# Streamed activation tiles of five matmul stages placed in groups at different 32-byte steps relative to the weight tiles

## What is computed

```python
def trunk_layer(...):
    h = rmsnorm(x, norm_mix)
    z = h @ w_in                      # projections of mixers A, B, C and of the merge gates
    o_a = dsa_attention(...); o_b = moba_attention(...); o_c = retention(...)
    m = (jax.nn.sigmoid(g_a) * (o_a @ w_pa) + jax.nn.sigmoid(g_b) * (o_b @ w_pb)
         + jax.nn.sigmoid(g_c) * (o_c @ w_pc))
    x = x + m @ w_out
    f, c_new = conv_ffn(rmsnorm(x, norm_ffn), cprev, ffn_up, ffn_gate, conv_w, conv_b, ffn_down)
    x = x + f

def conv_ffn(...):
    u, g = h @ ffn_up, h @ ffn_gate
    # c: causal convolution of width 3 over u
    y = (jax.nn.gelu(c, approximate=False) * g) @ ffn_down
```

## The kernel before

| jobs | weights | streamed | chunks x jobs | triples |
|---|---|---|---|---|
| pa | w_pa | oa_hi, oa_lo | 8 x 16 | 128 |
| pb | w_pb | ob_hi, ob_lo | 8 x 16 | 128 |
| out | w_out | m_hi, m_lo | 16 x 16 | 256 |
| d1 | ffn_down | y_hi, y_lo | 22 x 16 | 352 |
| d2 | ffn_down | y_hi, y_lo | 21 x 16 | 336 |

## Time and profile before

### The profile page before, as it was taken

How to read it: one execution, slowest core, us unless ns; L and a number is a source line. 1 busy time by engine, 2 the same in 40 slices (tenths; PEclk the granted TensorE clock), 3 DMA queues, 4 the chain that set the end, 5 groups by cost and what they waited for, 6 DMA issues and landing times.

```text
span 2383.5 us, 44504 instructions
## 1 busy us (share of the span) xinstructions
PE 2351.6 (99%) x17202; PEld 2270.1 (95%) x17202; DVE 1410.9 (59%) x2095; ACT 919.1 (39%) x1274; POOL 314.0 (13%) x629
## 2 busy tenths in 40 slices
PE   8999999999999999999999999999999999999997
PEld 8978999999999999998999999999999999999997
DVE  6535568989987545445456645666654356666443
ACT  5334444333333444334333344333333333333332
POOL 1135110000002322333200011000000000000001
PEclk9999999999999999999999999999999999999999
DMA  7448645546557988998776544444445544444553
GB/s 239 143 132 243 178 140 182 180 168 207 204 175 264 307 290 292 302 336 298 245 265 194 183 151 148 153 153 149 152 151 153 150 157 154 148 153 154 149 153 106
DMA packets 174434, 458.69 MB, mean 192 GB/s; under 512 B 25018, under 2 KB 74538, under 8 KB 174096
## 3 DMA queue, kind: packets, MB, share of 16 engines
q1 hardware_dynamic: 141040, 372.31, 47.9%
q0 software_dynamic: 26128, 75.67, 9.7%
q10 hardware_dynamic: 7056, 7.88, 0.9%
HBM read 425.27 MB, written 27.52 MB: 190 GB/s over the span
## 4 chain that ended last, share of the span: by engine, by line
PE 95%; DVE 2%; ACT 1%; issue 1%; DMA 0%; DVEq 0%; SPq 0%; ACTq 0%
PE ps L789 87%; PE ps L1061 1%; PE ps L1014 1%; PE ps L860 1%; PE ps L1044 1%; ACT w_hi L1102 1%; DMA xT<-in_x 0%; PE ps L984 0%; PE ps L976 0%; PE ps L872 0%; PE ps L927 0%; PE ps L963 0%; PE ps L967 0%; PE ps L824 0%; PE ps L902 0%
## 5 line engine op out<-in xcount | busy, mean ns | idle before, releaser
L1353 DVE TENSOR_TENSOR w_lo<-w_raw,w_hi 128x1024 fp32r<-128x1024 f32 (+1 forms) x622 | 749.4, 1207 | 778.3 <-ACT w_hi L1102 775.3
L789 PE MATMUL ps<-h_hi,w_hi 128*128 128x320 f32 x3696 | 1160.6, 314 | 11.7 <-DVE w_lo L1353 9.5
L789 PE MATMUL ps<-h_lo,w_hi 128*128 128x320 f32 x3696 | 1132.3, 306 | 0.0
L789 PE MATMUL ps<-h_hi,w_lo 128*128 128x320 f32 x3696 | 1125.8, 305 | 0.0
L1102 ACT ACTIVATE w_hi<-w_raw 128x1024 fp32r<-128x1024 f32 (+1 forms) x622 | 647.4, 1043 | 802.2 <-PE ps L789 790.5
L789 PEld LDWEIGHTS ps<-h_hi,w_hi 128*128 128x128 f32 x3696 | 694.7, 188 | 41.9 <-issue 38.9
L789 PEld LDWEIGHTS ps<-h_lo,w_hi 128*128 128x128 f32 x3696 | 694.9, 188 | 0.4
L789 PEld LDWEIGHTS ps<-h_hi,w_lo 128*128 128x128 f32 x3696 | 694.5, 188 | 0.0
L789 PE MATMUL ps<-y_hi,w_hi 128*128 128x320 f32 x688 | 213.5, 310 | 1.7 <-DVE yt L1425 1.7
L789 PE MATMUL ps<-y_lo,w_hi 128*128 128x320 f32 x688 | 210.5, 306 | 0.0
L789 PE MATMUL ps<-y_hi,w_lo 128*128 128x320 f32 x688 | 209.2, 304 | 0.0
(11 more groups left out here) (322 smaller groups left out, 2063.4 us busy)
## 6 DMA issues: line engine op xcount, KB each, us to landing
w_raw<-in_w_in SPq DMA_DIRECT2D x258, 512.0 KB, 5.0
w_raw<-in_ffn_up SPq DMA_DIRECT2D x86, 512.0 KB, 3.9
w_raw<-in_ffn_gate SPq DMA_DIRECT2D x86, 512.0 KB, 3.7
w_raw<-in_ffn_down SPq DMA_DIRECT2D x80, 448.0 KB, 3.4
kpg<-in_cache_b_k SPq DMA_DIRECT2D x128, 128.0 KB, 4.5
vpg<-in_cache_b_v POOLq DMA_DIRECT2D x128, 128.0 KB, 5.0
kpg<-in_cache_a_k SPq DMA_DIRECT2D x128, 128.0 KB, 4.8
vpg<-in_cache_a_v POOLq DMA_DIRECT2D x128, 128.0 KB, 4.9
```

The costliest lines, as they stand in the source:

```text
L789: mm = mmul(bank[q][:, 0:T], wp[:, s, cols], xp[:, x.k0 + k, :], start=(x.first and k == 0 and t == 0), stop=(x.last and k == x.nk - 1 and ...
L1353: tt(w_lo[:, s, 0:n], w_raw[:, s, 0:n], w_hi[:, s, 0:n].bitcast(F32), ALU.subtract).then_inc(w_lo_done, 1)
```

## The change

The tiles `oa`, `ob`, `m` and `y`, high part and rest, are no longer one tile each. Each is cut along k into groups (lots), and each group starts at a place of its own; a table `STEPS` gives for each group its chunks and the places of high part and rest. A helper `stepped` moves the start up to the next byte offset with the wanted place, allocates the group, and hands back a list of the chunks by k, which the matmuls and the makers of the chunks index. The weights and `h_hi`/`h_lo` stay where they are.

`oa_hi`, `oa_lo`, `ob_hi` and `ob_lo` are now made by two instructions of 1,280 elements each in place of one of 2,560. All other instructions keep their order and sizes. `x1`, `ost`, `sq`, `sqa`, `term` and the tables of the ConvFFN move by the bytes that the gaps take.

```diff
+STEPS = {"m": (((0, 6), 64, 0), ((6, 11), 96, 32), ((11, 16), 32, 32)),
+         "oa": (((0, 4), 64, 96), ((4, 8), 64, 32)),
+         "ob": (((0, 4), 96, 96), ((4, 8), 32, 96)),
+         "y": (((0, 5), 96, 0), ((5, 10), 32, 0), ((10, 16), 0, 96), ((16, 22), 0, 32))}
...
+        assert R % 128 == 0
+
+        def stepped(src, part, start, end):
+
+            by_k, by_lot = [], []
+            for (k0, k1), *steps in STEPS[src]:
+                start += (steps[part] - start) % 128
+                name = f"{src}_{('hi', 'lo')[part]}{k0}"
+                x = at(start, end)(name, [P, k1 - k0, T], F32R)
+                start += 4 * T * (k1 - k0)
+                by_k += [x[:, k, :] for k in range(k1 - k0)]
+                by_lot.append((k0, k1, x[:, :, :]))
+            return by_k, by_lot, start
...
-        oa_hi, oa_lo = ro("oa_hi", [P, 8, T], F32R), ro("oa_lo", [P, 8, T], F32R)
-        misc_at = ro.at - R
-        ob_hi, ob_lo = ro("ob_hi", [P, 8, T], F32R), ro("ob_lo", [P, 8, T], F32R)
-        x1_at = ro.at - R
-        x1 = ro("x1", [P, KD, T])
+        oa_hi, oa_hi_lots, end = stepped("oa", 0, ring_at + 32, 109376)
+        oa_lo, oa_lo_lots, misc_at = stepped("oa", 1, end, 109376)
+        ob_hi, ob_hi_lots, end = stepped("ob", 0, misc_at, 109376)
+        ob_lo, ob_lo_lots, x1_at = stepped("ob", 1, end, 109376)
+        x1 = at(x1_at, x1_at + 20480)("x1", [P, KD, T])
...
-        m_hi = at(0, 20480)("m_hi", [P, KD, T], F32R)
-        m_lo = at(ring_at + 32, ring_at + 20512)("m_lo", [P, KD, T], F32R)
-        rq = at(109376, 114496)
+        m_hi, _, _ = stepped("m", 0, 0, 20832)
+        m_lo, _, end = stepped("m", 1, ring_at + 32, misc_at + 512)
+        rq = at(x1_at + 20480, x1_at + 25600)
...
-        y_hi = at(0, 28160)("y_hi", [P, KF1, T], F32R)
-        y_lo = at(28160, 56320)("y_lo", [P, KF1, T], F32R)
-        rf = at(misc_at, x1_at)
+        y_hi, _, y_mid = stepped("y", 0, 0, misc_at)
+        y_lo, _, _ = stepped("y", 1, y_mid, misc_at)
+        rf = at(misc_at + 512, x1_at)
...
-                            mm = mmul(bank[q][:, 0:T], wp[:, s, cols], xp[:, x.k0 + k, :],
+                            mm = mmul(bank[q][:, 0:T], wp[:, s, cols], xp[x.k0 + k],
...
-                fn((oa_hi, ob_hi)[m][:, :, :], ost[:, m, :, :], ACT.Copy).then_inc(rounded, 1)
+                for k0, k1, x in (oa_hi_lots, ob_hi_lots)[m]:
+                    ins = fn(x, ost[:, m, k0:k1, :], ACT.Copy)
+                ins.then_inc(rounded, 1)
...
-                tt((oa_lo, ob_lo)[m][:, :, :], ost[:, m, :, :], (oa_hi, ob_hi)[m][:, :, :].bitcast(F32), ALU.subtract)\
-                    .then_inc(split, 1)
+                for (k0, k1, lo), (_, _, hi) in zip((oa_lo_lots, ob_lo_lots)[m], (oa_hi_lots, ob_hi_lots)[m]):
+                    ins = tt(lo, ost[:, m, k0:k1, :], hi.bitcast(F32), ALU.subtract)
+                ins.then_inc(split, 1)
```

More of the change, by code:

```diff
@@ L391, in build @@
         W = {n: a[n] for n in ("w_in", "w_pa", "w_pb", "w_pc", "w_out", "ffn_up", "ffn_gate", "ffn_down")}
-        X = {"h": (h_hi, h_lo), "oc": (h_hi, h_lo), "h2": (h_hi, h_lo), "oa": (oa_hi, oa_lo), "ob": (ob_hi, ob_lo),
+        by_k = tuple([x[:, k, :] for k in range(KD)] for x in (h_hi, h_lo))
+        X = {"h": by_k, "oc": by_k, "h2": by_k, "oa": (oa_hi, oa_lo), "ob": (ob_hi, ob_lo),
              "m": (m_hi, m_lo), "y": (y_hi, y_lo)}
@@ L1110, in evacuated @@
                     act.wait_ge(m_done, job.n + 1)
-                    fn(m_hi[:, job.n, :], m_f[:, job.n, :], ACT.Copy).then_inc(rounded, 1)
+                    fn(m_hi[job.n], m_f[:, job.n, :], ACT.Copy).then_inc(rounded, 1)
                 elif job.kind == "out":
@@ L1119, in evacuated @@
                     act.wait_ge(bank_free, j + 1)
-                    fn(y_hi[:, job.n % KF1, :], yt[:, job.n % 2, :], ACT.Copy).then_inc(rounded, 1)
+                    fn(y_hi[job.n % KF1], yt[:, job.n % 2, :], ACT.Copy).then_inc(rounded, 1)
                 elif job.kind == "d2":
@@ L1436, in later @@
                     dve.wait_ge(rounded, BEFORE["m"] + n + 1)
-                    tt(m_lo[:, n, :], m_f[:, n, :], m_hi[:, n, :].bitcast(F32), ALU.subtract).then_inc(split, 1)
+                    tt(m_lo[n], m_f[:, n, :], m_hi[n].bitcast(F32), ALU.subtract).then_inc(split, 1)
                 elif job.kind == "up":
@@ L1458, in later @@
                     i = n % KF1
-                    tt(y_lo[:, i, :], yt[:, n % 2, :], y_hi[:, i, :].bitcast(F32), ALU.subtract).then_inc(split, 1)
+                    tt(y_lo[i], yt[:, n % 2, :], y_hi[i].bitcast(F32), ALU.subtract).then_inc(split, 1)
             def dense(n):
```

## The result

The changed kernel takes 2390.65 us (median of 14 runs, 2389.57 to 2391.87) where the kernel before, run beside it on the same chip, takes 2385.52 us. The ratio is 1.0022, with a 95% interval of 1.0015 to 1.0029: slower, by 5.1 us (0.2%). The forecast had +1.1 us; the measured time lies inside the stated range, on the side of the slower rival.

A forecast was written before the change was run, and what follows sets the result against it. TensorE's matmul pace was taken as the bound. Terms 1.2 - 0.2 - 0.2 + 0.25 = +1.1 us on the profiled 2383.5 gave 2384.6, with 1.6 us around the span 2386.2 us; stated range 2381 to 2392 us.

The forecast's parts named there:

- slower rival: Streaming from 32 or 96 is itself bad, costing 8 us in d1, d2, out and pa: 2393.5 us; chance 0.24.
- That only relative places count: For all matmuls, cost depends on the streamed tile's place less the loading weights' place; no separate size.
- The price by pairs: Each matmul of y, m, oa costs c(d), d being streamed place less loading place; c from 143.8 to 147.1 ns.
- the new groups contain no d outside these four: Place differences d in the new groups are only 0, 32, 64 or 96, so the old trace can price them.
- The term for y: In d1 and d2, four groups of y, 688 triples at 433.3 ns before, sum to +1.2 us.
- that for m: In out, three groups of m, 256 triples at 436.7 ns before, sum to -0.2 us.
- that for oa: In pa, two groups of oa, 128 triples at 440.0 ns before, sum to -0.2 us.
- the sign that the prediction gave itself: In the changed timeline, one group over 3 ns a triple from its predicted pace would show the rule wrong.
- the bounds of the gaps: Outside pb, 1,616 matmuls streaming from 32 or 96: -8 us at a gap of 0.14, +8 us at 0.15.
- Additivity: In every stage a triple costs the sum 2 c(d_hi) + c(d_lo), fixed by its places; 433.3 to 440.0 ns before.
- The cover of pb: In pb, VectorE and ScalarE set 3.64 us a unit, so ob's groups count nothing; -0.3 us without that.
- The cut instructions: Four more instructions making oa and ob delay a TensorE unit by 0.25 us, bounds 0 and 0.5 us.

The follow-up runs named there:

- run with other places: Changed kernel with another set of group places for y, m, oa and ob; no total time given, y's groups took 438.8, 444.7, 439.9 and 444.3 ns a triple.
- first map: Changed kernel with each w_hi slot 32 bytes further than the last, w_lo at 128 modulo 256, and y, m, oa, ob in 15 groups; 2405.29 us.

## Why the prediction was right or wrong

**What bounds the kernel** was right: TensorE's pace, read from starts. The 5.4 us are its paces and one late unit.

**That only relative places count** was right (the move of everything). The slower rival had the sign, and +8.3 us where 5.1 came, but a wrong mechanism: a tile at 32 or 96 is not bad by itself. Its 0.24 rested on a reason that one run removes.

**The price by pairs failed**, and the step that failed is the sentence "the new groups contain no d outside these four". It holds modulo 128. The place counts modulo 256, and there eight differences are possible; of y's four groups none had both parts at a difference seen before. The term for y was 1.2 us and measured 3.85, that for m -0.2 and measured +1.25, that for oa -0.2 and measured 0. What misled was that four values of d for three equations looked like a full table, while in the kernel before the streamed tiles all lay in one half of 256 bytes and the weights in the other, so that nothing in its trace could tell 128 from 256. By the sign that the prediction gave itself, a group over 3 ns from its price, the rule is wrong in six groups of eleven (five up, one down). The forecast's own range should have reached to the bounds of the gaps from the start.

**Additivity**, the other assumption, fails as well: a triple at one and the same placement has no one price. In the run with other places, y's first group (96 above w_hi, 128 above w_lo, modulo 256) runs all of job 2 of d1 at 433.3 ns with gaps of 148, 140 and 146 ns, and job 4 of d2 at 440.0 ns with 147, 146 and 147, at identical places. The first map shows the same in units of h, and there the gaps of the triple just ahead go with the pace that follows. That what runs ahead decides is the reading of this; no run varied it alone. A table of prices by place can't hold it.

**The cover of pb held.** Its stretch took 57.5 us before and after, though ob's groups moved by -0.1 and -6.6 ns a triple.

**The cut instructions** cost 0.22 to 0.23 us for the 0.25 of the sum.

**The rule of the Trainium skill** (page "TensorE: Matmul & The Clock Gate", section "Step-by-step: what each phase is for") says that loading the next tile's weights takes no read bandwidth from the running matmul. The prediction's reading of it, that all places would be alike, is refuted: pa takes 440.0 or 433.3 ns a triple by its distance to the weight tiles. So the load and the stream are not independent here; whether it is read bandwidth that is lost, no run shows.

**The size.** That the stated range held the time is luck as far as the mechanism goes: it had been stretched into rivals of which neither was true. The forecast's own range, 2384 to 2388.5, did not hold the time, and its +1.1 us was a fifth of what came.

## What to carry to other kernels

When a kernel is bound by TensorE's pace, take the paces of its stages from starts: stages of the same shapes that differ by a few ns a matmul are a question of layout. Put all streamed tiles at the remainder of the best stage, relative to the weights, and fix that remainder modulo 256, not 128 (shown here for fp32r matmuls with 320 columns); a gap that aligns a tile modulo 128 can move it into the other half. A layout is cheapest judged on one stage in one trace, where 0.1 ns a triple can be read, and not on the total, where 1.4 us of 2385 are lost.

## What the runs showed of the hardware that was not expected

- A move of one streamed tile by 128 bytes changed the pace of its matmuls from 433.3 to 440.0 ns a triple (688 triples, +4.7 us of time); a move of everything by 32 bytes changed nothing.
- The paces that repeat triple for triple come in steps: 433.3, 436.7, 440.0 and 446.3 to 447 ns, which at 2.4 GHz are 1,040, 1,048, 1,056 and about 1,072 cycles, multiples of 8. Other arrangements alternate (y's last group takes 432 and 441 ns by turns) or repeat every three triples (434, 436 and 437 ns in h of the first map, mean 435.5), so means lie between the steps. Why the steps are these, and what collides, no run here shows.
- The surcharge over the stream is the same for three matmuls, with their three loads, of 320 columns and of 256: 33.3 ns.
- The same placement can run at two steady paces, 433.3 and 440.0 ns; which of them goes with the gaps of the triple ahead (82 units of h in the first map).
